# Delta stage attention: forget sums and causal mask added by TensorE in the score banks, and dummy products ahead of idle waits

## The chip, the cores and the metric

The kernel runs on one core of one Trainium2 chip. The metric is the device time of one execution in microseconds. TensorE (PE) multiplies, VectorE (DVE) and ScalarE (ACT) do the elementwise work, SyncE (SP) issues the DMAs. TensorE's clock is granted at one of two levels, 1.2 or 2.4 GHz; the profile gives it as a share of full speed.

## What is computed

Two transformers of two layers each, one behind the other, on 256 tokens of width 1024, all in float32. A layer of the first one has a mixer of three parts: a gated delta rule, a convolution and a "forgetting" attention of 6 heads. Layer 0 is followed by a dense feed-forward, layer 1 by eight experts of which each token takes two (the MoE stage). The second transformer has an attention with grouped heads (GQA) in its first layer and one with low rank projections (MLA) in its second. The part that the change rewrites is this attention:

```python
def forgetting_attention(q, k, v, log_f):
    c = jnp.cumsum(log_f.astype(f32), axis=1)
    ...
        s = jnp.einsum('bhqd,bhkd->bhqk', q_blk, kt) + cq_blk[..., None] - ck[:, :, None, :]
        s = jnp.where(key_pos[None, :] <= q_pos[:, None], s, -jnp.inf)
        p = jax.nn.softmax(s, axis=-1)
        return jnp.einsum('bhqk,bhkd->bqhd', p, vt)
```

To each score it adds the sum of the log forget gates from key to query, and it masks keys that lie behind the query.

## The kernel before

Each engine has one program, written out in order by hand; semaphores join them (`take` waits, `link` signals and waits for its own instruction). There is no scheduler: the order of the source is the order of the queue. Weights stream through a ring of six slots of 1 MB, which SP refills as the tiles that used a slot are done. PSUM is two tensors of four banks, `P0` (projections and attention outputs) and `P1` (everything else). A layer of the first transformer (`for l in range(2)`) runs on PE: 25 projection tiles `in`, mixed with transposes and Gram products of the delta rule; the inversion in five levels; the state loop of four chunks (from L799); `intra`; the turn of the delta rule's output (L831), which waits for DVE's `delta_out` (L1748) and is read by DVE at L1752 (`delta_read`); then `attention(FOX_PAIRS, ...)`, and the projection `out` (L497, called by `linear_normed`).

`attention` works on pairs of heads: six pairs, of which those with t = 0 have scores of width 128 (queries 0 to 127) and those with t = 1 of width 256. For pair p PE issues `scores(p)` (L608, two matmuls, one in rows 0 to 63 of the array and one in rows 64 to 127), `values(p-3)` (L618) and the transposes `flip(p-2)` (L627). DVE takes the row maximum of each of the two units (L1544), then moves an output (`put`, L1764), then divides the probabilities of pair p-1 (L1554, L1555). ACT takes the exponentials (L1113) and copies the turned probabilities out of PSUM (L1121). In the delta stage DVE's `prep` first adds the forget sums from `cc` and `CR` (L1759) and the mask `neg` (L1760) and writes the scores to SBUF (`SC`), from where the maximum and the exponential read them. In GQA and MLA the same `attention` has no `prep`: both read the bank.

`cc` (sums by query, a column for each head) and `CR` (sums by key, the same in all partitions) come from PE at L707 to L711 between the projection tiles, and DVE copies them at L1648 and L1649.

Elsewhere PE waits for a norm: for the standard deviation and the scaled rows (`rms_std`, then `both_ready` or `one_ready`) ahead of `gin`, `fup0`, `min` and `fup1`; for the last layer norm ahead of the squares that open the second transformer (`square_of`, L576); and for the routing table (`x_rows`, `row_map`) ahead of the gathers of the MoE stage (L877). The MoE stage streams its weights in 84 chunks of 4 MB into two buffers; chunk c+2 is issued when chunk c has been used.

In the profile a float32 matmul has two PE records, and a transpose one.

## Time and profile before

| | us |
|---|---|
| median of 3 runs | 3163.26 (3161.17 to 3167.71) |
| the profiled execution's own time | 3154.97 |
| its span | 3153.2 |
| mean granted TensorE clock | 0.962 of full speed |
| PE busy | 2884.5 (91%) |
| DVE busy | 1501.0 (48%) |
| ACT busy | 1137.2 (36%) |
| PE weight load busy | 1871.4 (59%) |

The span runs from the first to the last instruction. A busy PE is not a PE at its peak: its matmuls overlap, and at the lower clock the same work is busy for longer. The page gives the granted clock in 40 slices, which is too coarse for waits of some microseconds; the windows view gives it for any stretch.

### The profile page before, as it was taken

What the parts mean: (1) busy time and instruction counts of PE and PEld (TensorE: products, weight loads), DVE (VectorE), ACT (ScalarE), POOL (GpSimd) and SP (SyncE); (2) the same over time, 40 slices, a digit from 0 to 9 for tenths busy, and PEclk for the clock granted to TensorE, in tenths of its full rate; (3) what the DMA queues carried; (4) which work ended last, traced back from release to release, by engine and by line L of the source; (5) the groups of instructions that cost most, each with busy time, mean ns of one, the idle gap of its engine ahead of it and who ended that gap; (6) DMA issues with size and microseconds to landing.
All of it is one profiled execution on the core that took longest, in us unless ns stands there. A gap on an engine that the chain in (4) does not pass through costs nothing.

```text
span 3153.2 us, 67929 instructions
## 1 busy us (share of the span) xinstructions
PE 2884.5 (91%) x26308; PEld 1871.4 (59%) x26308; DVE 1501.0 (48%) x4806; ACT 1137.2 (36%) x3085; POOL 0.2 (0%) x4
## 2 busy tenths in 40 slices
PE   8979999978998989888988888989999999899998
PEld 7858887856555545555555554444444444557887
DVE  5641004564566666666666664783322200454321
ACT  3121002221566656565666652262211100243210
POOL 0000000000000000000000000000000000000000
PEclk9979999988999999999999998999999999999999
DMA  5444434364799999999999980101122211211441
GB/s 204 173 174 160 157 137 147 134 241 139 230 332 330 333 327 335 328 332 329 327 336 332 327 303 28 66 15 41 58 75 80 80 67 67 91 44 57 158 147 67
DMA packets 205858, 576.06 MB, mean 183 GB/s; under 512 B 6496, under 2 KB 6624, under 8 KB 179040
## 3 DMA queue, kind: packets, MB, share of 16 engines
q1 hardware_dynamic: 205536, 571.72, 52.5%
q8 instruction: 208, 3.41, 0.4%
q14 instruction: 114, 0.93, 0.1%
HBM read 570.65 MB, written 1.05 MB: 181 GB/s over the span
## 4 chain that ended last, share of the span: by engine, by line
PE 59%; DMA 21%; DVE 12%; issue 3%; ACT 3%; DVEq 1%; SPq 1%; ACTq 0%
PE P L497 44%; DMA ring<-ws_moe 20%; DVE arena L1894 4%; PE P L925 2%; DVE ring L1894 2%; PE P L686 1%; PE P L544 1%; PE P L608 1%; DVE small L1544 1%; PE P L618 1%; PE P L627 1%; DVEq L1891 1%; PE P L877 1%; PE P L576 1%; PE P L976 1%
## 5 line engine op out<-in xcount | busy, mean ns | idle before, releaser
L497 PE MATMUL P<-arena,ring 128*128 128x256 f32 (+1 forms) x2784 | 900.3, 484 | 24.7 <-ACT arena L1175 24.6
L497 PEld LDWEIGHTS P<-arena,ring 128*128 128x128 f32 x2784 | 531.9, 192 | 383.0 <-issue 335.4
L925 PE MATMUL P<-arena 128*32 128x256 f32 x6496 | 372.5, 381 | 6.0 <-DMA arena<-ws_moe 5.2
L925 PE MATMUL P<-ring,arena 128*32 128x256 f32 x4256 | 277.1, 409 | 75.6 <-DMA ring<-ws_moe 74.2
L497 PE MATMUL P<-X_sb,ring 128*128 128x256 f32 x1504 | 335.1, 384 | 2.2 <-ACT X_sb L1154 1.6
L497 PEld LDWEIGHTS P<-X_sb,ring 128*128 128x128 f32 x1504 | 287.5, 192 | 44.8 <-issue 3.1
L925 PEld LDWEIGHTS P<-arena 128*32 128x32 f32 x6496 | 215.0, 111 | 146.8 <-DMA arena<-ws_moe 9.7
L1894 DVE COPY arena<-ring 128x256 f32 x1008 | 211.6, 294 | 143.8 <-DMA ring<-ws_moe 138.8
L1377 ACT ACTIVATE arena<-ring 128x256 f32 x672 | 215.8, 406 | 170.0 <-DMA ring<-ws_moe 161.7
L925 PEld LDWEIGHTS P<-ring,arena 128*32 128x32 f32 x4256 | 148.7, 117 | 185.9 <-DMA ring<-ws_moe 86.7
L1894 DVE COPY arena<-arena 128x256 f32 x1008 | 211.8, 294 | 75.6 <-DMA arena<-ws_moe 58.4
L1377 ACT ACTIVATE arena<-arena 128x256 f32 x672 | 214.1, 403 | 72.9 <-DMA arena<-ws_moe 59.8
L925 PE MATMUL P<-arena,MIX 128*32 128x256 f32 x3360 | 192.0, 379 | 3.5 <-DMA arena<-ws_moe 2.9
L2038 DVE SCALAR_TENSOR_TENSOR arena<-P,pv,arena 128x510 f32<-128x510 f32 (+1 forms) x88 | 54.2, 616 | 290.1 <-ACT arena L1425 201.5
L1950 DVE SCALAR_TENSOR_TENSOR X_sb<-P,mod,X_sb 128x256 f32<-128x256 f32 x48 | 23.2, 484 | 296.7 <-PE P L497 296.1
L925 PE MATMUL P<-ring,MIX 128*32 128x256 f32 x2016 | 128.5, 402 | 37.5 <-DMA ring<-ws_moe 29.4
L925 PEld LDWEIGHTS P<-arena,MIX 128*32 128x32 f32 x3360 | 114.3, 110 | 73.3 <-issue 5.8
L497 PE MATMUL P<-MIX,ring 128*128 128x256 f32 (+1 forms) x512 | 147.1, 444 | 2.2 <-issue 2.2
L1894 DVE COPY ring<-ring 128x256 f32 x504 | 107.2, 294 | 68.0 <-DMA ring<-ws_moe 66.6
L1377 ACT ACTIVATE ring<-ring 128x256 f32 x336 | 108.8, 406 | 85.0 <-DMA ring<-ws_moe 80.2
L1165 ACT ACTIVATE arena<-X_sb 128x512 f32<-128x512 f32 (+1 forms) x40 | 21.0, 541 | 309.8 <-DVE X_sb L1950 309.8
L1894 DVE COPY ring<-arena 128x256 f32 x504 | 107.1, 294 | 47.1 <-DMA arena<-ws_moe 39.2
(360 smaller groups left out, 2652.6 us busy)
## 6 DMA issues: line engine op xcount, KB each, us to landing
ring<-ws_moe SPq DMA_DIRECT2D x84, 2048.0 KB, 14.2
arena<-ws_moe SPq DMA_DIRECT2D x84, 2048.0 KB, 15.2
ring<-ws_b SPq DMA_DIRECT2D x137, 1024.0 KB, 4.8
ring<-ws_a SPq DMA_DIRECT2D x67, 1024.0 KB, 4.9
cst_sb<-cst SPq DMA_DIRECT2D x1, 1664.0 KB, 8.5
X_sb<-xT SPq DMA_DIRECT2D x1, 1024.0 KB, 4.9
X_sb<-ctxT SPq DMA_DIRECT2D x1, 1024.0 KB, 4.7
out<-Y SPq DMA_DIRECT2D x2, 512.0 KB, 2.6
```

The lines of the kernel that those rows point to most:

```text
L497: ins = nc.tensor.matmul(bank(i, n), blockap(s, b % SLOT), rhs(kk), start=kk == 0, stop=kk == k - 1)
L544: ins = nc.tensor.matmul(P0[32 * j:32 * j + 32, b, 256 * half:256 * half + 256], csil[:, k, :], w, start=k == 0, stop=k == KD - 1)
L576: ins = nc.tensor.matmul(P1[:, 0, 0:n], c_("ones"), SQH[:, k, 0:n], start=k == 0, stop=k == KD - 1)
L608: nc.tensor.matmul(P1[:, (2 * p + i) % 4, 0:nk * P], q, kk, start=True, stop=True)\
L618: ins = nc.tensor.matmul(P0[i * HD:(i + 1) * HD, p % 2, 0:P], vfn(h + i, j), ptb[:, (2 * p + i) % 4, j * P:(j + 1) * P], start=j == 0, sto ...
L627: ins = nc.tensor.transpose(P0[:, 2 + i, j * P:(j + 1) * P], pb[:, (2 * p + i) % 6, j * P:(j + 1) * P], c_("ident"))
L686: ins = nc.tensor.matmul(P1[c:c + HD, 2 * i + h, r * HD:(r + 1) * HD], lhs[c:c + HD, g], cident[c:c + HD] if rhs is None else rhs[c:c + HD ...
L877: ins = nc.tensor.matmul(gathered(n)[:, 0:w], XTM[:, t, k * P:(k + 1) * P], SEL[:, t, at:at + w], start=t == 0, stop=t == TT - 1)
L925: ins = nc.tensor.matmul(acc(g // 2)[BR * j:BR * (j + 1), g % 2], x[:, b * BR:(b + 1) * BR], weights_of(b), start=k == 0, stop=last and kk ...
L1377: ins = a.activation(CB[u % 3][:, NDVE + j].rearrange("p (h c) -> p h c", h=2), src, ACT.Copy)
L1894: ins = v.tensor_copy(CB[u % 3][:, j].rearrange("p (h c) -> p h c", h=2), src)
L2038: L(v.scalar_tensor_tensor(f3[:, :, 1:], b3[:, :, 0:T - 1], pv[:, w0 + 3 * m:w0 + 3 * m + 1], f3[:, :, 1:], ALU.mult, ALU.add))
```

## The change

Four edits.

1. The forget sums and the mask go into the score banks on PE. Behind each score matmul, which no longer closes its accumulation, come a product of `ident` with `neg` on the last 128 columns and a product of two rows, `past_l` with `past_r`. The two rows are (-1, c of the query) and (c of the key, 1), so their product is c of the query less c of the key. DVE's `prep`, `SC`, `cc` and `CR` are gone, and maximum and exponential read the bank, as in GQA. The three small products for `cc` go, DVE copies 2 partitions in place of 128 for the key sums, and ACT makes the two operands from them with two activations of 2 x 1536 elements in the state loop.
2. The banks of this attention are rotated by two (`fox_bank`), so the first pair uses banks 2 and 3 of `P1`, and the scores of pair 0 are issued ahead of the turn of the delta rule's output, which moves into `attention` as `between`.
3. Unread products `busy(to, n)`: n matmuls of `ones` with `cos64`, 256 columns, into a part of a bank that nobody reads. They stand ahead of the waits for `delta_out` (6, in both layers), for the routing table (12), for the squares that open the second transformer (14), and for `rms_std` ahead of `gin` (10), `fup0` (10), `min` (10) and `fup1` (7).
4. Buffers in `arena` move to make room (not shown).

```diff
+        def fox_bank(u):
+            return P1[:, (u + 2) % 4]
...
+            def busy(to, n):
+
+                for _ in range(n):
+                    nc.tensor.matmul(to, c_("ones"), c_("cos64", T), start=True, stop=True)
...
-            def attention(pairs, qk, vfn, pb, ptb):
+            def attention(pairs, qk, vfn, pb, ptb, bias=None, between=None):
...
-                        nc.tensor.matmul(P1[:, (2 * p + i) % 4, 0:nk * P], q, kk, start=True, stop=True)\
-                            .then_inc(sem("scores"), 1)
+                        to = fox_bank(2 * p + i) if bias else P1[:, (2 * p + i) % 4]
+                        ins = nc.tensor.matmul(to[:, 0:nk * P], q, kk, start=True, stop=bias is None)
+                        if bias:
+                            ins = bias(to, h + i, t, nk)
+                        ins.then_inc(sem("scores"), 1)
...
                 for p in range(n + 3):
                     if p < n:
                         scores(p)
+                    if p == 0 and between:
+                        between()
...
-                nc.tensor.matmul(P1[:, 3, 0:6], c_("tri"), lft[:, 0], start=True, stop=True)
-                nc.tensor.matmul(P1[:, 3, 6:12], c_("tri"), lft[:, 1], start=True, stop=False)
-                nc.tensor.matmul(P1[:, 3, 6:12], c_("ones"), lft[:, 0], start=False, stop=True)
...
-                C.take("delta_out")
-                for r in range(6):
-                    ins = nc.tensor.transpose(P1[:, r // 3, r % 3 * P:(r % 3 + 1) * P],
-                                              O1[:, 2 * r:2 * r + 2, :].rearrange("p g d -> p (g d)"), c_("ident"))
-                ins.then_inc(sem("delta_flipped"), 1)
-                C.take("delta_read")
-                C.take("mod_ready", 6)
+
+                def forget(to, h, t, nk):
+
+                    nc.tensor.matmul(to[:, (nk - 1) * P:nk * P], c_("ident"), c_("neg"), start=False, stop=False)
+                    return nc.tensor.matmul(to[:, 0:nk * P], past_l[:, h, t * P:(t + 1) * P], past_r[:, h, 0:nk * P],
+                                            start=False, stop=True)
+
+                def delta_flip():
+
+                    for m in range(25 - NBANK, 25):
+                        if (TILE[f"in{l}"] + m) % NBANK == 3:
+                            wait_out(pe, TILE[f"in{l}"] + m)
+                    busy(P0[:, 3, 0:T], 6)
+                    C.take("delta_out")
+                    for r in range(6):
+                        ins = nc.tensor.transpose(P1[:, r // 3, r % 3 * P:(r % 3 + 1) * P],
+                                                  O1[:, 2 * r:2 * r + 2, :].rearrange("p g d -> p (g d)"), c_("ident"))
+                    ins.then_inc(sem("delta_flipped"), 1)
+                    C.take("delta_read")
+                    C.take("mod_ready", 6)
...
-                          lambda h, j: foxV[:, j, h * HD:(h + 1) * HD], foxP, foxPT)
+                          lambda h, j: foxV[:, j, h * HD:(h + 1) * HD], foxP, foxPT, forget, delta_flip)
...
+                    busy(P1[:, 0, T:2 * T], 12)
                     C.take("x_rows", 2)
...
+            busy(P1[:, 3, 0:T], 14)
             for k in range(KD):
                 x_wait(k)
...
             for l in range(2):
+                busy(P1[:, 1, 0:T], 10)
                 C.take("rms_std")
...
                     linear_squared("gout", KD, both(MIX), n)
+                    busy(P1[:, 1, 0:T], 10)
                     C.take("rms_std")
...
                     linear_squared("mout", KD, lambda k: mix1[:, k, :], T)
+                    busy(P1[:, 1, 0:T], 7)
                     C.take("rms_std")
...
+                    if n == 1:
+                        A.link(a.activation(past_r, past_l, ACT.Identity, scale=c_("ident", 1)[0:2], bias=second))
                     if n == 2:
+                        A.link(a.activation(past_l, past_l, ACT.Identity, scale=second, bias=less_first))
...
-                attention(FOX_PAIRS, lambda u, w: SC[:, u % 4, 0:w], foxP, foxPT)
+                attention(FOX_PAIRS, lambda u, w: fox_bank(u)[:, 0:w], foxP, foxPT)
...
-                L(v.tensor_copy(cc.rearrange("p t c -> p (t c)"), P1[:, 3, 0:12]))
-                L(v.tensor_copy(CR.rearrange("p h t -> p (h t)"), P1f[:, 0:1536]), "forget_read")
+                L(v.tensor_copy(past_l.rearrange("p h t -> p (h t)"), P1f[0:2, 0:1536]), "forget_read")
...
-                def prep(u, h, t, w):
-
-                    dst = SC[:, u % 4, 0:w]
-                    L(v.scalar_tensor_tensor(dst, P1[:, u % 4, 0:w], cc[:, t, h:h + 1], CR[:, h, 0:w], ALU.add, ALU.subtract))
-                    L(v.tensor_tensor(SC[:, u % 4, w - P:w], SC[:, u % 4, w - P:w], c_("neg"), ALU.add))
-                    return dst
-
-                attention(FOX_PAIRS, prep, foxP,
+                attention(FOX_PAIRS, lambda u, h, t, w: fox_bank(u)[:, 0:w], foxP,
```

PE in layer 0 from `intra` to the third pair's scores, before (L686 `intra`, L553 turns modulation rows, L831 turns the delta output, L608 scores, L627 `flip`):

```order
L686 MATMUL P<-arena 64x64 x24
L553 MATMUL P<-cst_sb,arena 128x96 x4
L831 MATMUL P<-cst_sb,arena 128x128 x6
L608 MATMUL P<-MIX 128x128 x2
L608 MATMUL P<-MIX 128x256 x2
L608 MATMUL P<-MIX 128x128 x2
L627 MATMUL P<-cst_sb,arena 128x128 x2
```

The same place now, up to the first unit of the second pair (L617 scores, L842 mask, L843 forget sums, L491 dummies, L854 the turn of the delta output):

```order
L699 MATMUL P<-arena 64x64 x24
L561 MATMUL P<-cst_sb,arena 128x96 x4
L617 MATMUL P<-MIX 128x128
L842 MATMUL P<-cst_sb 128x128
L843 MATMUL P<-arena 128x128
L617 MATMUL P<-MIX 128x128
L842 MATMUL P<-cst_sb 128x128
L843 MATMUL P<-arena 128x128
L491 MATMUL P<-cst_sb 128x256 x6
L854 MATMUL P<-cst_sb,arena 128x128 x6
L617 MATMUL P<-MIX 128x256
L842 MATMUL P<-cst_sb 128x128
```

The first pair's scores and the dummies now stand ahead of the turn, and between the two score matmuls of a pair stand a mask and a forget product.

DVE in the same stretch, before (L1748 writes `delta_out`, L1522 modulation, L1752 reads the turned output):

```order
L1748 TENSOR_TENSOR arena<-arena,small 128x768
L1522 TENSOR_TENSOR mod<-P,pv 128x2x3x2 x2
L1752 SCALAR_TENSOR_TENSOR MIX<-P,pv,Y 128x384 x2
L1759 SCALAR_TENSOR_TENSOR arena<-P,small,arena 128x128
L1760 TENSOR_TENSOR arena<-arena,cst_sb 128x128
L1544 TENSOR_REDUCE small<-arena 128x1
L1759 SCALAR_TENSOR_TENSOR arena<-P,small,arena 128x128
L1760 TENSOR_TENSOR arena<-arena,cst_sb 128x128
L1544 TENSOR_REDUCE small<-arena 128x1
```

And now:

```order
L1780 TENSOR_TENSOR arena<-arena,small 128x768
L1554 TENSOR_TENSOR mod<-P,pv 128x2x3x2 x2
L1784 SCALAR_TENSOR_TENSOR MIX<-P,pv,Y 128x384 x2
L1576 TENSOR_REDUCE small<-P 128x1 x4
L1586 RECIPROCAL small<-small 128x1
L1587 TENSOR_SCALAR arena<-arena,small 128x128
```

Of three instructions for a unit one is left; the four maxima of the first two pairs stand in a row.

## Rows read from the trace of the kernel before

**Rows 1.** Windows: stretch, length, busy by engine (records), granted clock, DMA share, GB/s.

```profile
194.12:221.05 26.93, 16.21 (x79) 9.13 (x79) 20.66 (x66) 9.69 (x36) 0.00 (x0) 0.50 0.00 1
221.05:231.30 10.25, 10.25 (x34) 8.50 (x35) 0.44 (x2) 0.00 (x0) 0.00 (x0) 0.70 0.00 0
722.12:731.30 9.18, 9.18 (x35) 7.84 (x36) 0.72 (x2) 0.00 (x0) 0.00 (x0) 0.81 0.00 0
```

**Rows 2.** Timeline, layer 0: start, duration, engine, line, operation, records [idle before <-releaser].

```profile
191.15 1.54 PE L831 MATMUL P<-cst_sb,arena 128*128 128x128 f32 x6 [4.62 <-DVE arena L1748]
192.79 1.27 DVE L1752 SCALAR_TENSOR_TENSOR MIX<-P,pv,Y 128x384 f32<-128x384 f32 x2 [1.29 <-PE P L831]
194.12 1.65 PE L608 MATMUL P<-MIX 64*128 64x128 f32 x8 [1.43 <-DVE MIX L1752]
...
200.73 0.35 DVE L1759 SCALAR_TENSOR_TENSOR arena<-P,small,arena 128x128 f32<-128x128 f32 x1
...
207.61 0.35 DVE L1759 SCALAR_TENSOR_TENSOR arena<-P,small,arena 128x128 f32<-128x128 f32 x1
...
221.05 10.20 PE L497 MATMUL P<-MIX,ring 128*128 128x256 f32 x32 [0.57 <-issue]
```

**Rows 3.** The chain that ended last, a stretch of projection tiles: start, length, records.

```profile
97.38 24.39 PE P L497 x112
```

**Rows 4.** Timeline, first work behind each wait; 1945.62 ends the first tile of `gin`.

```profile
785.38 13.05 PE L877 MATMUL P<-Y 128*128 128x512 f32 x32 [7.28 <-DVE Y L1842]
...
1922.25 9.49 PE L576 MATMUL P<-arena,cst_sb 128*128 128x512 f32 x16 [7.98 <-ACT arena L1165]
...
1937.60 16.01 PE L497 MATMUL P<-arena,ring 128*128 128x512 f32 x32 [5.85 <-ACT arena L1175]
...
1945.62 0.30 PEld L497 LDWEIGHTS P<-arena,ring 128*128 128x128 f32 x2 [0.88 <-ACT arena L1175]
...
2225.84 16.45 PE L497 MATMUL P<-arena,ring 128*128 128x512 f32 x32 [6.13 <-ACT arena L1175]
...
2695.14 4.03 PE L497 MATMUL P<-arena,ring 128*128 128x256 f32 x8 [6.13 <-ACT arena L1175]
...
2904.77 11.50 PE L497 MATMUL P<-arena,ring 128*128 128x256 f32 x40 [4.63 <-ACT arena L1175]
```

**Rows 5.** Groups by line, 194 to 221.1 us: count, busy us, mean ns, idle before.

```profile
L1759 DVE SCALAR_TENSOR_TENSOR arena<-P,small,arena 128x128 f32<-128x128 f32 (+1 forms) x12 | 5.0, 418 | 1.3 <-PE P L608 1.0
...
L1760 DVE TENSOR_TENSOR arena<-arena,cst_sb 128x128 f32<-128x128 f32 x12 | 3.5, 292 | 0.4
...
L1764 DVE TENSOR_SCALAR MIX<-P,pv 128x128 f32<-128x128 f32 x6 | 2.1, 351 | 3.2 <-PE P L618 3.1
```

**Rows 6.** Row maxima by tile (ns min/median/max), and score starts of the GQA attention, timeline.

```profile
L1544 DVE TENSOR_REDUCE small<-P x96: 424/691/693, 2056.0 to 2858.3; 128x1 f32<-128x512 f32 x64, 128x1 f32<-128x256 f32 x32
...
2070.42 1.13 PE L608 MATMUL P<-arena 64*128 64x512 f32 x4
...
2082.37 1.13 PE L608 MATMUL P<-arena 64*128 64x512 f32 x4
```

**Rows 7.** Timeline, forget sums of layer 0 and ACT rows near the new activations.

```profile
39.84 0.28 PE L707 MATMUL P<-small,cst_sb 128*128 128x6 f32 x2
...
40.43 2.82 PE L711 MATMUL P<-arena,cst_sb 128*128 128x512 f32 x6
...
41.74 0.84 ACT L1203 ACTIVATE arena<-arena 128x768 f32<-128x768 f32 x1
...
176.54 0.48 ACT L1294 ACTIVATE arena<-P 64x384 f32<-64x384 f32 x1 [6.46 <-PE P L807]
```

**Rows 8.** Window ahead of the issue of the fourth weight chunk of the MoE stage.

```profile
824.00:828.00 4.00, 4.00 (x80) 2.91 (x76) 4.00 (x21) 4.00 (x14) 0.00 (x0) 1.00 0.02 4
```

**Rows 9.** Windows in the routing of the MoE stage, columns as in rows 1.

```profile
775.60:776.10 0.50, 0.50 (x4) 0.50 (x3) 0.41 (x3) 0.00 (x0) 0.00 (x0) 0.50 1.13 324
...
777.00:778.00 1.00, 1.00 (x11) 0.92 (x10) 0.28 (x2) 0.97 (x2) 0.00 (x0) 1.00 0.99 268
```

More of the change, by code:

```diff
@@ L229, in build @@
         MT = [YD, bd(8)]
-        CR = arena_at(19968, 1536).rearrange("p (h t) -> p h t", h=H1)
+        past_l = arena_at(19968, 1536)[0:2].rearrange("p (h t) -> p h t", h=H1)
+        past_r = arena_at(0, 1536)[0:2].rearrange("p (h t) -> p h t", h=H1)
         foxA = FM.rearrange("p k r t -> p (k r t)")[:, 0:1536]
@@ L267, in build @@
         lft = small[:, 324:336].rearrange("p (t c) -> p t c", t=TT)
-        cc = small[:, 336:348].rearrange("p (t c) -> p t c", t=TT)
         rt = small[:, 352:512]
@@ L1566, in _ @@
             L(v.memset(rms_eps, RMS_EPS))
+            L(v.tensor_scalar(less_first, c_("ident", 1)[0:2], -1.0, None, ALU.mult))
             for g, ng in neg_gain.items():
```

6 lines of the change are left out of this document (3 added, 3 removed).

## The prediction

> **What bounds the kernel now.** PE is busy for 91% of the span, so the places matter in which it waits or runs at the low clock. First the windows view over the attention of the delta stage. In layer 0 it lasts 26.93 us from the first scores to the first matmul of `out`; DVE is busy for 20.66 us of it and PE for 16.21, and the granted clock is 0.50 throughout, which is 1.2 GHz [rows 1]; layer 1 issues the same instructions and is taken to be alike. The timeline shows why: PE had stood for 4.62 us before the turn of the delta output, then 1.43 us more, and every later burst is short [rows 2]. The `out` projection that follows runs its first 32 records in 10.20 us [rows 2], at a mean clock of 0.70, and in layer 1 the clock over that stretch is 0.81 [rows 1]. At full clock a 256 column record takes 24.39 / 112 = 0.218 us [rows 3], so 32 records would be 7.0 us.
>
> Then the waits of PE that get dummies, each with the work behind it [rows 4]. A low clock behind a wait costs time only where PE has its operands and runs dense work; where it waits for rows of the norm anyway it costs none.
>
> **The change part by part.**
>
> *Steady part of the attention.* From the third pair to the fifth DVE takes 207.61 - 200.73 = 6.88 us for two pairs, four units [rows 2], with next to no idle time in front of its groups [rows 5]. `prep` is 0.418 + 0.292 us a unit [rows 5], and about 0.78 with the gaps between instructions. Without it two pairs take 6.88 - 4 x 0.78 = 3.8 us, and with two `put` of 0.35 [rows 5], which that stretch does not yet hold, 4.5. The maximum now reads PSUM: 0.424 us for 256 elements [rows 6], where it was 0.42 from SBUF, so nothing there.
>
> PE gets for two pairs four mask products of 128 columns and four forget products, two of 128 and two of 256 columns. At full clock a matmul of two records is 0.22 us for 128 columns and 0.43 for 256 [rows 3]. The two score matmuls of a pair, which ran side by side in two halves of the array, now have others between them. That makes 1.1 us for a narrow pair's scores and 1.7 for a wide one's; with values (0.7) and transposes (0.7) some 4.2 us for two pairs at 2.4 GHz and 8.3 at 1.2 GHz. A product of only two rows is not in the trace. I price it like a full one; were it free, 1.3 us would go for two pairs, and it can't add more than its columns unless PSUM accumulation costs extra, which the long accumulations of `out` don't show.
>
> With DVE at 4.5 and PE at 4.2 neither is saturated, and what is late next is the loop across the engines: scores, two maxima, two exponentials, two copies, values, transposes, scores of the pair after next. I laid out the six pairs with the durations of the rows, each engine in its order. Scores of the odd pairs start at 0, 3.7 and 8.4 us behind the reading of the turned output, the last output is moved at 15.8 and `out` starts near 16.6 at full clock. The same layout gives 25.8 at 1.2 GHz, because PE is then the bound. Laid out for the kernel before it gives 26.4 where the trace has 26.93 [rows 1], and for four pairs of the GQA attention, which has no `prep`, 11.9 where the trace has 2082.37 - 2070.42 = 11.95 [rows 6]. So the gain lies between 1.1 and 10.3 us a layer. I take 8.6: nearly the full clock, since PE is busy 85% of the loop, with one stretch of some 3 us at the low one, most likely in the thin last 6 us.
>
> *The start.* PE now does the first scores and six dummies (1.1 + 6 x 0.43 = 3.7 us) ahead of `delta_out`, so 0.9 us of the 4.62 remain idle [rows 2], and the turn should be at full clock: its six records of 128 columns at 0.11 us in place of 0.22, some 0.85 us for 1.54 [rows 2, 3]. Gain 0.7 a layer, 1.4 in all; between 0 and 1.5.
>
> *`out` behind it.* Its low clock costs 3.2 us in layer 0 and, from 0.81 over 9.18 us [rows 1], 1.9 in layer 1. If the attention ends at full clock all 5.1 come back. The last 6 us are thin, so I take half: 2.6, between 0 and 5.1.
>
> *Forget sums.* L707 to L709 take 40.43 - 39.84 = 0.59 us of a busy PE [rows 7]: 1.1 in both layers, between 0 and 1.2. DVE's copy of 1536 elements stays as long with 2 partitions as with 128; its copy to `cc` was beside PE's work. ACT gets two activations of 1536 elements in each state loop. 768 took 0.84 us [rows 7], so 1.6 each. Behind them in ACT's queue is the copy L1294, which PE waits for in turn, but that copy stood idle for 6.46 us before [rows 7], so they cost nothing; uncovered they would be 6.4 us.
>
> *Dummies outside.* A dummy is 0.43 us at full clock. Ahead of the gathers 12 take 5.2 of 7.28 us; ahead of the squares 14 take 6.0 of 7.98; ahead of `gin` 10 take 4.3 of 5.85; ahead of `fup0` and `min` 4.3 of 6.13; ahead of `fup1` 7 take 3.0 of 4.63 [rows 4]. All fit if the clock is at 2.4 GHz when they start, and leave 1.5 to 2.1 us. What a full clock behind them gives: the gathers are 16 matmuls, half of 512 and half of 256 columns, 10.3 us for 13.05, gain 2.7. The squares are 16 records of 512 columns, 7.1 us for 9.49, gain 2.3. The 40 records of `fup1` take 11.50 for 8.9 at full clock, but at that clock its first tile would wait for rows of the norm, so of these 2.6 I take 1.7. In the first tile of `gin` PE, though it began at the low clock, stood 0.88 us for its last rows [rows 4], so a full clock gives nothing there, nor in `min`, whose matmuls are half as wide behind the same rows; in `fup0` I take 0.2. Sum 6.9, between 0 and 7.8.
>
> *Does it pass through the MoE stage?* It is bound by DMA later, but at its start the DMA engines stand (share 0.02) until chunk 1 is used [rows 8], so a PE that comes there earlier starts the stream earlier by as much.
>
> *Sum.* 17.2 + 1.4 + 2.6 + 1.1 + 6.9 = 29.2 us. Against the profiled execution's own 3154.97 that is 3125.8; the median of the runs shown lies 8.3 higher, so 3163.26 - 29.2 = 3134.
>
> **A rule weighed.** In the routing of the MoE stage PE ends a row of 16 transposes (L861) at a clock of 0.50, and a microsecond behind them, with only 8 column matmuls and four more transposes in between, the clock is 1.00 [rows 9]. So here transposes went ahead of a rise. The Trainium skill, "TensorE: Matmul & The Clock Gate", section "Part 4: PE-mode transpose", says that full speed does not engage for transposes and that they do not count as busy work in the same way. By that rule the turn and the `flip` records would not help to hold the clock in the attention, which makes rival A likelier; by the row they do. The trace disagrees with the rule, if one rise can; I leave a part of A's chance to it.
>
> **Rivals.**
>
> A. *PE takes DVE's place as the bound of the attention at 1.2 GHz.* The mask and forget products double PE's load, and the clock was 0.50 for the whole stretch. Against it: PE would then be busy nearly all the time, and in the trace dense work brings the clock up: the squares lose 9.49 - 7.1 = 2.4 us, five or six of their 16 records, and then run at full speed [rows 4]. Gain 2 x 1.1 + 1.1 + 1.4 + 6.9 = 11.6, so 3152.
>
> B. *The dummies don't hold the clock over the 1.5 to 2.1 us that remain,* or the products are not counted as they seem. Then the 6.9 are gone: gain 22.3, so 3141.
>
> C. *The MoE stage swallows what is saved ahead of it,* because its DMA would set its end from an earlier point. Only squares, `fup0` and `fup1` are left: 4.2, so 3159. Against it stands the idle DMA [rows 8].
>
> D. *Slower: dummies that run at 1.2 GHz outlast the waits they fill.* At 0.86 us each they take 12.0 us of 7.98 ahead of the squares, 10.3 of 7.28, 8.6 of 5.85, of 6.13 and of 6.13, 6.0 of 4.63: 4.1 + 3.0 + 2.7 + 2.5 + 2.5 + 1.4 = 16 us, and 2.5 in each attention, 21 in all. With the gains of A inside, 3.3, the kernel takes 3181. It decides from the point where a wait is shorter than its dummies, 9 low clock dummies for the squares. Against it: all these waits follow dense work, and at the one before the gathers the clock reads 1.00 a microsecond ahead [rows 9].
>
> **How the numbers follow.** Forecast 0.66 (with 0.04 for more than 35 us), A 0.10, B 0.17, C 0.04, D 0.03. A difference of 0.2%, 6.3 us, is about what a measurement of this kernel can tell from no change. Faster: forecast, A and B, 0.93; same: C, 0.04; slower: D, 0.03. The range: at best 2 x 10.3 + 1.5 + 5.1 + 1.2 + 7.8 = 36.2, so 3127, and 3 us for the scatter of the runs, 3124. Above it reaches over B and B with a weaker attention (gain 15), 3148; A, C and D, 0.17, are left out.
>
> **What would show it.** In the profile after: the first PE record of `out` 16.5 to 18.5 us behind the reading of the turned output; clock near 1.00 over most of it and DVE no longer continuous; the turn at 0.8 us; gathers near 10.3, squares near 7.1, the first 16 records of `fup1` with small gaps in them; 32 records of `out` between 7 and 10.2. A clock of 0.50 in the attention with PE busy without gaps speaks for A; 13.05 and 9.49 unchanged for B; the end of the MoE stage unmoved for C; first real matmuls later than `x_rows` or `rms_std` for D. The weakest step is how long the clock holds through the thin end of the attention.

## The result, and the profile after

The changed kernel is slower: 3177.97 us (median of 7 runs, 3168.98 to 3183.18) against 3165.18 for the kernel before in the same group of runs, a ratio of 1.0034 with an interval of [1.0023, 1.0046]. Forecast was 3134. Its profiled execution took 3183.01 us with a span of 3180.9; that is a long draw of after beside a short one of before (3154.97), so the two traces differ by 27.7 us where the medians differ by 12.8.

The page of the changed kernel: engines with busy time, share and instructions, and the granted clock in 40 slices.

```profile
PE 2961.9 (93%) x26542; PEld 1919.5 (60%) x26542; DVE 1483.4 (47%) x4757; ACT 1143.3 (36%) x3089; POOL 0.2 (0%) x4
...
PEclk9979999997999999999999999999999999999999
```

DVE lost 18 us of work, as meant, and PE gained 77 us. Where they went shows in the windows over the attention of layer 0, from the first scores behind the turn to `out`, over the first records of `out`, over the attention of layer 1, and over the "dummies" (the unread products of the change) and the gathers (columns as in [rows 1]).

```profile
197.03:235.17 38.14, 36.25 (x114) 20.61 (x115) 12.19 (x42) 9.64 (x36) 0.00 (x0) 0.51 0.00 0
...
235.17:245.00 9.83, 9.83 (x37) 8.31 (x38) 0.84 (x2) 0.00 (x0) 0.00 (x0) 0.80 0.01 2
705.00:743.60 38.60, 35.29 (x121) 20.23 (x119) 13.44 (x44) 9.69 (x36) 0.00 (x0) 0.57 0.00 1
...
800.70:808.45 7.75, 7.75 (x26) 6.36 (x25) 6.51 (x22) 0.00 (x0) 0.00 (x0) 0.68 1.02 336
808.45:818.80 10.35, 10.31 (x32) 5.73 (x31) 1.27 (x3) 2.45 (x5) 0.00 (x0) 1.00 0.67 231
```

The stretch that took 26.93 us [rows 1] takes 38.14. DVE's share fell from 20.66 to 12.19 us; PE is busy for 36.25, and the clock is 0.51 (0.50 before). The timeline of PE says what one unit costs (columns as in [rows 2]).

```profile
194.78 0.82 PE L854 MATMUL P<-cst_sb,arena 128*128 128x128 f32 x6
197.03 0.70 PE L617 MATMUL P<-MIX 64*128 64x256 f32 x2 [1.43 <-DVE MIX L1784]
197.66 0.49 PE L842 MATMUL P<-cst_sb 128*128 128x128 f32 x2
198.08 1.20 PE L843 MATMUL P<-arena 2*128 2x256 f32 x2
199.21 1.22 PE L617 MATMUL P<-MIX 64*128 64x256 f32 x2
200.36 0.79 PE L842 MATMUL P<-cst_sb 128*128 128x128 f32 x2
201.08 1.22 PE L843 MATMUL P<-arena 2*128 2x256 f32 x2
202.23 0.79 PE L617 MATMUL P<-MIX 64*128 64x128 f32 x2
202.95 0.79 PE L842 MATMUL P<-cst_sb 128*128 128x128 f32 x2
203.68 0.79 PE L843 MATMUL P<-arena 2*128 2x128 f32 x2
204.40 0.79 PE L617 MATMUL P<-MIX 64*128 64x128 f32 x2
```

The turn ran at full clock (0.82 us for 1.54 [rows 2]) and so did the first two products behind it. From 198.1 the starts are 1.15 us apart behind 256 columns and 0.72 behind 128, without an idle record. A wide unit, score, mask and forget product, costs 202.23 - 199.21 = 3.02 us, a narrow one 204.40 - 202.23 = 2.17. Its columns alone would be 2.1 us for a wide unit at this clock (products of 256, 128 and 256 columns, by the 0.436 us that 256 columns take at full clock, 24.39 / 56 [rows 3]); the other 0.9 us are three times 0.29, and a weight load (LDWEIGHTS) takes 0.30 us there. The stretch holds three wide and two narrow pairs, 3 x 6.04 + 2 x 4.34 = 26.8 us. With the values (L629, 5.5 us) and transposes (L638, 5.4 us), here from the groups by line of that stretch, this count gives 37.7 us, a little more than the 36.25 busy, since the first unit began at full clock. So PE's queue alone fills the attention.

```profile
L842 PEld LDWEIGHTS P<-cst_sb 128*128 128x128 f32 x20 | 4.8, 297 | 4.5 <-issue 4.5
L629 PE MATMUL P<-arena 128*64 128x128 f32 x36 | 5.5, 439 | 1.3 <-ACT arena L1150 1.3
L638 PE MATMUL P<-cst_sb,arena 128*128 128x128 f32 x18 | 5.4, 439 | 0.0
```

DVE now waits for it (its timeline).

```profile
202.41 0.42 DVE L1576 TENSOR_REDUCE small<-P 128x1 f32<-128x256 f32 x1 [2.60 <-PE P L843]
```

In the table "attention" runs from DVE's reading of the turned output to `out`; for the kernel before that is 221.05 - 192.79 = 28.3 [rows 2]. It follows the two traces by their landmarks.

| stretch | before, us | after, us | difference |
|---|---|---|---|
| start to the reading of the turned output, layer 0 | 192.8 | 195.7 | +2.9 |
| attention, layer 0 | 28.3 | 39.5 | +11.2 |
| `out` to the reading, layer 1 | 472.7 | 470.6 | -2.1 |
| attention, layer 1 | 28.3 | 37.8 | +9.5 |
| `out` to the gathers | 63.3 | 64.7 | +1.4 |
| gathers and the MoE stage | 1123.0 | 1129.2 | +6.2 |
| norm, squares, to `gin` | 29.3 | 28.6 | -0.7 |
| `gin` to `fup0` | 288.2 | 288.1 | -0.1 |
| `fup0` to `fup1` | 678.9 | 680.0 | +1.1 |
| `fup1` to the end | 248.4 | 246.7 | -1.7 |
| sum | | | +27.7 |

The attention is 20.7 of it. The MoE stage, whose code the change leaves as it is, took between 1119.5 and 1133.1 us in the fourteen traces of this study. Most of that lies between groups of runs: 1128.1 to 1133.1 us in the four traces of the first group of experiments, 1127.1 to 1130.5 in the four of the next, 1119.5 to 1123.6 in the three after that. The reading in layer 0 came at 192.8 to 196.1 us in the four traces whose kernels don't differ up to there. So the 6.2 and the first 2.9 are within what traces differ by anyway. That leaves 18.6 us, 4 more than the upper end of the interval (1.0046, 14.6 us); these 4 are not placed. One way would be that other executions of the changed kernel had the low clock for a shorter part of the attention, as one kernel below has in one layer and not in the other; there are no traces of them.

### The profile page after: what moved, and what is told of

The parts are those of the page before. It is cut to its first block, busy times and chain, and to the rows that moved or that the text cites. A ratio compares the mean times of both kernels' runs of the same rounds, so it can differ in the third digit from the quotient of the medians.

```text
span 3180.9 us, 68352 instructions
## 1 busy us (share of the span) xinstructions
PE 2961.9 (93%) x26542; PEld 1919.5 (60%) x26542; DVE 1483.4 (47%) x4757; ACT 1143.3 (36%) x3089; POOL 0.2 (0%) x4
## 4 chain that ended last, share of the span: by engine, by line
PE 60%; DMA 21%; DVE 11%; issue 3%; ACT 3%; DVEq 1%; SPq 1%; ACTq 0%
PE P L505 44%; DMA ring<-ws_moe 21%; DVE arena L1919 4%; PE P L950 2%; DVE ring L1919 2%; PE P L617 2%; PE P L699 2%; PE P L552 1%; PE P L629 1%; PE P L638 1%; DVEq L1916 1%; DVE small L1576 1%; PE P L584 1%; PE P L901 1%; PE P L1001 1%
## 5 line engine op out<-in xcount | busy, mean ns | idle before, releaser
L950 PE MATMUL P<-ring,MIX 128*32 128x256 f32 x2016 | 130.8, 407 | 35.9 <-DMA ring<-ws_moe 29.3
```

The costliest lines, as they stand in the source:

```text
L950: ins = nc.tensor.matmul(acc(g // 2)[BR * j:BR * (j + 1), g % 2], x[:, b * BR:(b + 1) * BR], weights_of(b), start=k == 0, stop=last and kk ...
```

## The experiments

The theory behind them: the loss is the price of the products in PE's queue, at a clock that they themselves keep low; the dummies outside are worth little. The rival: the dummies are a part of the loss.

**The dummies outside alone.** The kernel before with them (`busy` as in the change):

```diff
+                    busy(P1[:, 0, T:2 * T], 12)
                     C.take("x_rows", 2)
...
+            busy(P1[:, 3, 0:T], 14)
             for k in range(KD):
                 x_wait(k)
```

> The kernel before with only the dummies outside the delta stage's attention (12, 14, 10, 10, 10, 7), the attention untouched. Theory 1, the loss sits in the attention and the dummies outside bring a little: in the trace of the changed kernel the gathers bring 2.7 - 1.6 = 1.1 us (their dummies end 1.6 later than the wait did), the squares 0.7, fup1 1.8, the others 0, min and mout cost up to 1.5: 2.5 to 3.6 us faster than before, so about 3162 on the median 3165, and the MoE stage takes the 1085.0 us of before. Theory 2, the dummies are part of the loss, because the MoE stage behind the gathers took 1093.8 us in place of 1085.0: 5 us slower than before, with the same 1094 in its trace.

Measured: 3161.27 us, ratio 0.9977 [0.9965, 0.9988]. The rival, slower, is out. In the trace squares, `fup1` and `min` are as in the changed kernel. The gathers are not; here they are beside those of two later kernels (grouped order, and 128 rows in the order of the change):

```profile
779.57 5.37 PE L488 MATMUL P<-cst_sb 128*128 128x256 f32 x24
787.01 12.25 PE L882 MATMUL P<-Y 128*128 128x512 f32 x32 [2.07 <-issue]
...
785.43 10.56 PE L904 MATMUL P<-Y 128*128 128x512 f32 x32 [0.54 <-issue]
...
782.00 10.56 PE L902 MATMUL P<-Y 128*128 128x512 f32 x32 [2.06 <-issue]
```

With the dummies outside alone they ended 2.07 us ahead of the gathers and these took 12.25 us, little less than the 13.05 of [rows 4]. In the changed kernel the dummies ran at 0.68, took 7.75 us and ended as the gathers began, which then took 10.48. There the gathers started 1.4 us later behind the transposes of the routing than in the kernel before; the dummies make some 0.65 of it (the gathers began 0.75 us behind DVE's last write to `Y`, 0.10 before), the rest came with the small products of the routing, which ran slower (0.57 us for 0.37). These two traces alone would say that a set is worth 0.8 to 1.2 us, not 2.7. The later ones say more: where the dummies began at the low clock and ended 0.53 to 0.56 us ahead (four kernels) the gathers took 10.56 us with no delay behind DVE, and in one kernel they took 10.56 with the same 2 us of idle PE that cost the clock here. So the full gain did come in most kernels, and a gap of 2 us can go either way. The MoE stage took 1133.1 us here, so beside that stage the trace gives 2.3 us for all the dummies (gathers 0.8, squares 0.7, `fup1` 1.8, `gin` 0.1, less 1.1 between `fup0` and `fup1`, where those ahead of `min` stand), and the ratio 3.8 to 11; what is above 2.3 is not placed.

**The attention alone.** The changed kernel without any `busy`.

> The changed kernel without any of its dummies, inside and outside the attention. Theory 1: the attention is bound by PE at 1.2 GHz, 38 us in place of 27, so two layers cost 2 x 11 us, less 1.1 for the forget sums and about 1 for the earlier scores: 18 to 21 us slower than before, 3185; the turn is back at 1.5 us and the attention as long as with the six dummies, since with them the clock fell 1.4 us behind the first score anyway. Theory 2 (the dummies are part of the loss): under 12 us slower, 3174 or less.

Measured: 3189.88 us, ratio 1.0074 [1.006, 1.0087]: 23 us slower than before, where the first theory had 18 to 21 and the second under 12. The first is the nearer one, and misses by 2 us. Attention 40.3 us in both layers, the turn 1.51 us.

**The mask alone on PE.** The kernel before, with

```diff
+                            ins = nc.tensor.matmul(to[:, (nk - 1) * P:nk * P], c_("ident"), c_("neg"), start=False, stop=True)
...
-                    L(v.tensor_tensor(SC[:, u % 4, w - P:w], SC[:, u % 4, w - P:w], c_("neg"), ALU.add))
```

> The kernel before with the mask alone added by PE (ident times neg, 128 columns, behind each of the 12 score matmuls of a layer); DVE still adds the forget sums, and loses the 12 instructions of 0.29 us (0.33 with the gap). Theory 1, each product costs PE 0.72 us at 1.2 GHz in sequence (0.43 of columns and 0.29 that nothing hides): PE goes from 16.2 to 24.9 us busy in a layer, DVE from 20.7 to 17.2, and the attention stays between 26 and 29 us, the kernel within 4 us of before. Rival, only the product of two rows is dear: the attention follows DVE down to 23 to 24 us, the kernel 6 to 8 us faster.

Measured: 3178.4 us, ratio 1.004 [1.0024, 1.0055]. Attention 33.4 and 33.7 us, 5.2 more than before on average, though DVE was busy for 3.5 us less (17.16 for 20.66). Both missed: the rival by its sign, mine because it left out what the mask does to its neighbours. The two score matmuls of a pair, in the upper and the lower 64 rows, no longer follow each other and no longer run side by side: a narrow pair's two, 0.80 us in the trace of before, become 4 x 0.72 = 2.9 with their masks, a wide pair's 1.23 become 2 x (1.15 + 0.72) = 3.7. Three of each are 13.8 us more, and PE's busy time went from 16.21 to 30.04 us:

```profile
195.50:227.50 32.00, 30.04 (x102) 18.08 (x102) 17.16 (x54) 9.85 (x36) 0.00 (x0) 0.50 0.00 1
```

**A probe.** Unread products behind the last work of the kernel before, each row behind an idle PE; one execution.

```diff
+            at(2)
+            for i in range(24):
+                ins = mm(q[i % 4][:, 0:T], two_l, two_r, start=True, stop=True)
+            end(ins)
...
+            at(4)
+            for i in range(20):
+                mm(q[i % 4][:, 0:T], on_, mv, start=True, stop=True)
+            for i in range(10):
+                half_score(i, T)
+                mm(q[i % 4][:, P:T], id_, c_("neg"), start=False, stop=False)
+                ins = mm(q[i % 4][:, 0:T], two_l, two_r, start=False, stop=True)
```

> The kernel before with ten rows of unread products behind its last work, each behind an idle time of more than 4 us of PE (ACT copies 1536 elements four times), so only prices and clock are read: 24 full ones of 256 columns; 32 of 128 columns; 24 of two rows and 256 columns; ten times a unit of the changed attention (64 rows x 256, 128 x 128, 2 rows x 256); the same behind 20 full ones without a gap; the unit with its last product of 128 rows; 24 of 64 rows in alternate halves; 64 transposes; the units of two heads with the products of a kind next to each other; 20 full ones and then 24 of two rows. Theory a, the unhidden 0.29 us comes where the number of rows or the half of the array changes from one matmul to the next: full ones 0.43 us at full clock, two-row ones alone 0.43, 128 columns 0.22 to 0.25, the unit 1.15 + 0.72 + 1.15 = 3.0 at 1.2 GHz and 1.8 at 2.4; with 128 rows in the last product it loses one such piece, 2.7. Theory b, it belongs to every short product: 128 columns alone cost 0.42. For the clock, theory c: it doesn't rise through the unit nor through two rows alone, and falls to 0.50 in the unit that stands behind 20 full ones without a gap; rival d: it falls only behind an idle time, so behind the 20 full ones the unit runs at 1.00 throughout, and from a cold start it rises as with full ones.

Timeline: full products of 256 columns, of 128, two rows, 64 rows in alternate halves, transposes, and two-row ones behind 20 full ones.

```profile
3166.20 13.48 PE L1112 MATMUL P<-cst_sb 128*128 128x256 f32 x48 [7.23 <-ACT arena L1560]
3185.85 8.94 PE L1116 MATMUL P<-cst_sb 128*128 128x128 f32 x64 [6.17 <-ACT arena L1560]
3200.96 20.84 PE L1120 MATMUL P<-cst_sb 2*128 2x256 f32 x48 [6.17 <-ACT arena L1560]
...
3342.31 7.30 PE L1145 MATMUL P<-cst_sb 64*128 64x256 f32 x48 [6.17 <-ACT arena L1560]
3355.79 9.11 PE L1150 MATMUL P<-cst_sb 128*128 128x128 f32 x64 [6.19 <-ACT arena L1560]
...
3410.27 16.89 PE L1165 MATMUL P<-cst_sb 2*128 2x256 f32 x48
```

Windows of PE (length, busy, clock): two rows alone; ten units of the changed attention; the same behind full ones, in four stretches; units with 128 rows in the last product; halves at their end; transposes at their start and at their end; two-row ones behind full ones.

```profile
3200.96:3221.80 20.84, 20.84 (x48) 0.50 0.00 1
3227.98:3258.00 30.02, 30.02 (x60) 0.50 0.00 0
...
3274.80:3276.30 1.50, 1.50 (x7) 1.00 0.00 0
3276.30:3277.80 1.50, 1.50 (x7) 1.00 0.05 11
3277.80:3279.40 1.60, 1.60 (x4) 0.51 0.00 0
3279.40:3302.50 23.10, 23.10 (x47) 0.50 0.00 0
3308.80:3336.00 27.20, 27.20 (x60) 0.50 0.00 0
...
3347.00:3349.60 2.60, 2.60 (x26) 1.00 0.00 0
...
3355.80:3359.00 3.20, 3.20 (x15) 0.50 0.00 0
...
3362.00:3364.90 2.90, 2.90 (x27) 1.00 0.00 0
...
3414.00:3427.00 13.00, 13.00 (x32) 0.51 0.00 0
```

On the clock, theory c holds and d falls. Two-row products never brought it up in 20.84 us of unbroken work, and behind full ones, with no gap, it was lost. The unit of the changed attention does the same. Full products, 64-row ones in alternate halves and transposes bring it up. On the price, theory a holds and b falls: 128 columns on the full array cost 8.94 / 32 = 0.28 us with their cold start, while the unit cost 3.02. But one part was not expected: the unit with 128 rows in its last product (2.72 us) stays at 0.50 too. With the products of a kind next to each other a wide pair costs 4.31 us, where the order of the change costs 6.04.

**Grouped order.** The changed kernel, with scores, masks and forget products of a pair each next to each other:

```diff
+                    for i in range(2):
+                        nc.tensor.matmul(to[i][:, (nk - 1) * P:nk * P], c_("ident"), c_("neg"), start=False, stop=False)
+                    for i in range(2):
+                        nc.tensor.matmul(to[i][:, 0:nk * P], past_l[:, h + i, t * P:(t + 1) * P], past_r[:, h + i, 0:nk * P],
+                                         start=False, stop=True).then_inc(sem("scores"), 1)
```

> The changed kernel with its products in another order: for a pair the two scores, then the two masks, then the two forget products, in place of score, mask, forget for the one head and then for the other. In the probe that order took 4.31 us for a pair of 256 columns where the changed order takes 2 x 3.02 = 6.04, both at 1.2 GHz. Theory, the loss comes from products that no longer run beside each other or hide their weight loads: 3 wide pairs save 1.73 each and 3 narrow ones about 1.2, 8.8 us a layer, so from the reading of the turned output to out 30 to 31 us in place of 39.5, the clock still 0.50 (the two rows are still there), and the kernel 17 us faster than the changed one, near 3161. Rival, the time is set by the clock alone and other engines take over as the limit: less than 4 us a layer.

Measured: 3155.94 us, ratio 0.9966 [0.9951, 0.9981]. Attention 26.8 us in layer 0, where the clock was 1.00 up to 200 us, and 31.7 in layer 1, where it was 0.63 from 691 to 695 us and 0.50 behind; the text expected 30 to 31 in both. The order of PE's products alone turns the change from 0.34% slower into 0.34% faster.

**DVE's share.** The kernel before with the mask put into the key sums beforehand, so `prep` is one instruction:

```diff
-                    L(v.scalar_tensor_tensor(dst, P1[:, u % 4, 0:w], cc[:, t, h:h + 1], CR[:, h, 0:w], ALU.add, ALU.subtract))
-                    L(v.tensor_tensor(SC[:, u % 4, w - P:w], SC[:, u % 4, w - P:w], c_("neg"), ALU.add))
+                    L(v.scalar_tensor_tensor(dst, P1[:, u % 4, 0:w], cc[:, t, h:h + 1], CR[:, h] if t else CRM[:, h],
+                                             ALU.add, ALU.subtract))
```

> The kernel before with the mask already in the sums that DVE subtracts: one DVE instruction for a unit in place of two, 12 of 0.33 us fewer in a layer; two DVE instructions of 768 elements in the state loop, in waits of 1.8 and 2.8 us. PE does what it did before. Theory, DVE bounds the attention of before: 28.3 us from the reading to out become 24.4 to 25, the kernel 7 us faster than before, 3159. Rival, the loop across the engines sets it at the low clock and DVE's share only fills it: 27 us or more, under 3 us faster.

Measured: 3152.68 us, ratio 0.9949 [0.9932, 0.9965]; attention 24.5 in both layers, 3.8 less each. So DVE did bound the attention of the kernel before, as the prediction read it, and the forecast of the attention failed on PE's side. The ratio says 11 us or more where the attention gives 7.6 (the text expected 7 in all); another 1.5 lie between `out` of layer 0 and the reading in layer 1, the rest is not placed.

**One product of 128 rows, and more dummies.** Grouped, with mask and forget sums in one product; `CR` and `CRM` hold the mask less the key sums:

```diff
+                    for i in range(2):
+                        nc.tensor.matmul(to[i][:, 0:nk * P], c_("ident"), CR[:, h + i] if t else CRM[:, h + i],
+                                         start=False, stop=True).then_inc(sem("scores"), 1)
```

> The changed kernel with all its dummies, but one product of 128 rows for mask and forget sums together (ident times a matrix that holds the mask less the key sums; the query's own sum is the same for a whole row and leaves the softmax as it is), the two scores of a pair next to each other and then the two products. DVE makes the matrices with three instructions of 768 elements in the state loop. Theory c, the clock follows how many rows of the array work: with no two-row product and the 64-row ones side by side it rises in the attention as it did in the probe for 64 rows in alternate halves and for transposes; reading to out 18 to 21 us, the last part of it near 1.00, out 7 to 9 us, the kernel 15 to 20 us faster than before, 3148. Rival, PE's waits decide and the clock stays 0.50: PE then needs 16.2 + 3 x (1.15 + 2.0) = 25.7 us a layer, reading to out 27 to 29, the kernel within 4 us of before.

Measured: 3132.6 us, ratio 0.9886 [0.9869, 0.9902]. Attention 19.8 us in both layers, the clock back at 1.00 from 205.6 us, `out` 7.14 us for its 32 records, which is full speed. The attention is as the text had it; the kernel gained 36 us, twice the 15 to 20 expected, of which the attention has 17.0 and `out` 4.8. The windows are a stretch at the low clock, the rest of the attention from where the clock is back, and `out`:

```profile
198.50:200.40 1.90, 1.90 (x5) 1.11 (x4) 0.42 (x1) 0.62 (x5) 0.00 (x0) 0.50 0.00 0
...
205.60:216.30 10.70, 8.37 (x70) 5.29 (x69) 7.90 (x28) 5.43 (x22) 0.00 (x0) 1.00 0.00 0
216.30:223.50 7.20, 7.20 (x34) 6.35 (x35) 0.45 (x2) 0.00 (x0) 0.00 (x0) 1.00 0.01 2
```

> As the kernel with one product of 128 rows for mask and forget sums, and with more dummies: 3 in the wait for the reading of the turned output and 13 in the attention, ahead of waits for exponentials and turned probabilities. Theory c: where the clock falls in the waits of the kernel without them, these hold it at 1.00 to the end, reading to out 17 to 19 us and out at 7.0, some 3 us a layer better than without. If the clock isn't held, they cost 16 x 0.86 = 14 us a layer at 1.2 GHz less the idle time they fill: reading to out over 30 us, slower than before.

Measured: 3139.64 us, ratio 0.991 [0.9893, 0.9927]. The clock is 1.00 from the reading to the end of `out`, and the attention is 20.7 us, 0.8 longer than with 0.50 in most of its first half, where the text had 17 to 19. The dummies did hold the clock, and they stood ahead of real work. The two effects part in the trace of the kernel without the dummies ahead of `gin`, `fup0` and `min` (below), whose attention is the same code as that with one product. In its layer 0 the clock stayed at 1.00, in its layer 1 it fell:

```profile
193.08:210.52 17.44, 13.52 (x95) 8.40 (x95) 13.45 (x44) 8.37 (x36) 0.00 (x0) 1.00 0.01 4
679.34:699.19 19.85, 16.20 (x95) 10.11 (x95) 13.44 (x44) 8.51 (x36) 0.00 (x0) 0.83 0.01 2
```

So a held clock was worth 2.4 us in a layer, and the 16 further dummies, with the waits moved for them, cost 3.2.

**Rows alone, in both orders.** The forget product over 128 rows, 126 of them zeros, all else as it was: first with the grouped order, then with the order of the change.

```diff
-                        nc.tensor.matmul(to[i][:, 0:nk * P], past_l[:, h + i, t * P:(t + 1) * P], past_r[:, h + i, 0:nk * P],
+                        nc.tensor.matmul(to[i][:, 0:nk * P], past_l_all[:, h + i, t * P:(t + 1) * P], past_r_all[:, h + i, 0:nk * P],
```

> The kernel with scores, masks and forget products grouped by kind, and the forget product over 128 rows in place of two: the same two rows and zeros in the other 126, in both operands (cleared by two memsets of DVE). The columns, the number and the order of PE's products are the same. Theory c, the clock follows the rows in use: it rises in the attention, which had 0.50 from 203 us on, and reading to out comes from 31.7 us (layer 1) to 22 to 25, out from 9.5 towards 7.1; the kernel 12 to 18 us faster than with two rows. Rival, it is the number and size of the products and the idle time between them: 0.50 as before, 30 to 32 us less the 0.29 a pair that an equal tile shape saves between mask and forget product, at most 1.8 us a layer.

Measured: 3124.43 us, ratio 0.9884 [0.9869, 0.9899], so 0.8% or 26 us from two rows to 128, beyond the 12 to 18 expected. Attention 19.2 and 20.8 us for 26.8 and 31.7, `out` 7.14 in both layers for 9.79 and 9.49: 23.5 us together. Layer 0 in windows:

```profile
196.00:199.00 3.00, 2.97 (x21) 2.23 (x21) 2.49 (x10) 1.68 (x9) 0.00 (x0) 1.00 0.01 3
199.00:202.00 3.00, 3.00 (x25) 2.09 (x25) 1.90 (x7) 1.57 (x6) 0.00 (x0) 1.00 0.00 0
202.00:205.00 3.00, 3.00 (x24) 1.95 (x24) 2.08 (x8) 1.14 (x6) 0.00 (x0) 1.00 0.00 0
```

The same products with two rows had 0.58 from 200 to 203 us and 0.50 behind. In PE's queue columns, number, order and waits are the same, and only the rows differ; DVE has two memsets more, ahead of the attention. So the clock follows the rows in use here. Equal rows of mask and forget product also save one unhidden 0.29 us a pair, which this pair of kernels doesn't part from the rows. The probe does: its two-row products by themselves take their columns and no more (20.84 / 24 = 0.87 us), and the clock stays down.

> The changed kernel with the forget product over 128 rows (126 of them zeros) and nothing else changed: the products of a pair stay in its order, score, mask, forget for the one head and then for the other. With the changed kernel, the grouped one and the grouped one with 128 rows this makes four cases, order by rows. By the probe the unit in this order costs 2.72 us at 1.2 GHz with 128 rows in its last product, and the clock did not rise in ten of them: so 0.50 stays, and a unit saves 0.30: reading to out 34 to 36 us, the kernel 6 us faster than the changed one, slower than or as fast as before, 3168. Rival, rows alone are enough in the kernel, since transposes and values stand between the units and the clock is at 1.00 when the first unit starts: 1.00 in most of the attention, reading to out 22 to 25 us, 30 us faster than the changed one, 3145.

Measured: 3149.48 us, ratio 0.9955 [0.9929, 0.9981]. Each text has one layer: layer 0 took 22.6 us, as the rival said, and layer 1 took 36.6, as the theory did (34 to 36) to within 1 us, both with six dummies ahead and the same instructions:

```profile
198.00:201.00 3.00, 3.00 (x15) 1.83 (x15) 1.75 (x6) 1.77 (x8) 0.00 (x0) 1.00 0.01 3
...
684.00:700.00 16.00, 16.00 (x47) 9.46 (x45) 5.41 (x19) 4.75 (x20) 0.00 (x0) 0.51 0.00 0
```

Its ten runs fall into clusters: three from 3128 to 3131 us, one at 3141, five from 3149 to 3152, one at 3159. In layer 1 the clock, once lost, didn't come back before `out`, which cost 14.0 us; that two, one or no such layer in a run explains the clusters is what one trace suggests, not what is shown.

**Fewer dummies.** The kernel with one product, without those ahead of `gin`, `fup0` and `min`, and without any.

> The kernel with one product of 128 rows for mask and forget sums, without the dummies ahead of gin, fup0 and min. By the trace of the kernel before with only the outside dummies these three bring nothing and the ones ahead of min cost 1.1 us: 1 us faster than with them, which the median can't show, 3131.6. Rival, they hold a clock that the work behind needs: 2 us slower or more.

> The same kernel without any dummies. Theory: the attention brings its own clock up, because after three pairs it is dense enough; only the turn (0.7 us a layer) and the outside dummies (2.7 us) are lost and some 1 us a layer in the first pairs: 6 us slower than with all dummies, 3139. Rival, the start at full clock is what lets the clock come back early: 0.50 to the end of the attention, 27 us from reading to out and out at 9.5 us, 20 us slower, 3153.

Measured: 3130.4 us, ratio 0.9909 [0.9896, 0.9923], and 3132.6 us, ratio 0.9912 [0.9898, 0.9925], beside the 3124.43 of the 128-row kernel in the same group of runs. Without the three sets it is as expected (3131.6), a difference that the runs can't show; without any, 3139 were expected. Without any dummies the attention is 18.9 us in both layers and its clock comes up by itself, in layer 0 as follows; `out` has 7.14 and 8.82 us, the gathers 13.04.

```profile
194.00:197.20 3.20, 3.17 (x10) 1.69 (x10) 1.01 (x3) 1.04 (x5) 0.00 (x0) 0.50 0.00 0
197.20:198.80 1.60, 1.60 (x9) 1.38 (x9) 1.30 (x5) 0.90 (x4) 0.00 (x0) 0.55 0.00 0
198.80:211.50 12.70, 10.45 (x80) 6.46 (x78) 9.91 (x35) 6.52 (x28) 0.00 (x0) 1.00 0.00 1
```

The kernel with the four sets left and the one with none lie 2.2 us apart in one group of runs, which can't be told from nothing. The one with all of them stands at 0.9886 [0.9869, 0.9902] in another group, 0.0026 or 8 us lower, with an interval that just touches. By the same comparison the three sets ahead of `gin`, `fup0` and `min` would be worth 7 us, where the trace of the outside dummies has them as a loss of 1 us, so two groups of runs may differ by as much. What all the dummies are worth is not shown, beyond that from end to end of the intervals it is at most 18 us.

| kernel | attention, layers 0 and 1, us | ratio to before |
|---|---|---|
| before | 28.3, 28.3 | 1 |
| changed: its order, 2 rows | 39.5, 37.8 | 1.0034 |
| its order, 128 rows | 22.6, 36.6 | 0.9955 |
| grouped, 2 rows | 26.8, 31.7 | 0.9966 |
| grouped, 128 rows | 19.2, 20.8 | 0.9884 |
| grouped, one product of 128 rows | 19.8, 19.8 | 0.9886 |
| the same without three sets of dummies | 17.4, 19.9 | 0.9909 |
| the same without any | 18.9, 18.9 | 0.9912 |

The grouped kernels with 128 rows beat the kernel before by 0.9 to 1.2%, and keep what the change wanted of DVE in the attention.

## Why the prediction was wrong

**The steady part of the attention** carried 17.2 of the 29.2 us, and its sign was wrong: +20.7. Two steps of it failed.

The price of a product. The text took 0.22 and 0.43 us, the columns alone, and for a wide pair 1.7 us at 2.4 GHz, so 3.4 at 1.2; the trace has 6.04. It had seen that the two score matmuls of a pair "now have others between them", but its sums don't hold it: 0.43 + 0.44 + 0.86 = 1.7, and 0.22 + 0.44 + 0.44 = 1.1 for a narrow pair, count the two scores once, as if still side by side. One after the other they make 2.2 and 1.3, or 4.3 for a wide pair at 1.2 GHz. And it had no term for the loading of weights. Between these products of unlike rows it shows: 0.29 us a product at 1.2 GHz, six of them in a pair, 1.7 us. So "it can't add more than its columns" was false, and for the 25.8 us of the layout at 1.2 GHz the trace has 38.14. A hint was within reach: the first two pairs' scores took 1.65 us [rows 2], where their columns, side by side at 1.2 GHz, make 0.43 + 0.85 = 1.28.

The clock. The text saw 0.50 throughout [rows 1] and argued that a PE busy for 85% of the loop would bring it up, from the squares, which use the full array. Busy time alone isn't the measure: with 36.25 us busy of 38.14 it stayed at 0.51. How many rows PE computes with in that time matters, and the two-row product that the text would "price like a full one" isn't one for the clock. Of the two steps this one turned the sign. In the order of the change, with 128 rows, the layer that kept 1.00 took 22.6 us, so the price by itself left 5.7 us of gain where 8.6 were forecast; the rest, to 39.5, is the clock, with the little that 128 rows save in price. And where both were mended, one grouped product and the clock at 1.00, the attention took 17.4 us, within the 16.5 to 18.5 that the prediction named: the layout across the engines was sound.

**The start**: the turn took 0.82 us as forecast, but the first pair's scores with their masks and forget products took 2.5 us ahead of it, not 1.1. So the dummies ended 0.5 us behind `delta_out`, and the reading starts 0.2 us earlier, not 0.7. **`out`**: 9.1 and 9.2 us for 32 records for 10.2 and 8.8, gain 0.8 in place of 2.6. **Forget sums**: right, 0.6 us a layer (L721 starts 8.9 us behind the end of the first 48 records, where L711 started 9.5 behind them). **Dummies outside**: 6.9 forecast, 2.7 in the trace of the change and 2.3 in that of the dummies alone. `fup1` was right (1.8). The squares gained 0.7 of 2.3 (8.80 us for 16 records), with 1.93 us between the last dummy and them. The gathers are told above. Between `fup0` and `fup1`, where those ahead of `min` stand, 1.1 were lost, where the text had a gain of 0.2.

**The MoE stage** did pass on what came later or earlier at its start, as far as its scatter of 14 us lets one see. That scatter is larger than most terms of the sum, and the text took the profiled run of before, its shortest, as if the 8.3 us between it and the median were a constant.

**The rivals.** A named the right thing, PE as the bound at 1.2 GHz, and gave it 0.10 and a gain, since its price came from the same wrong layout. B was right in the main for the squares, in all traces, and for the gathers in the trace of the outside dummies alone. D, dummies that outlast the wait, came true ahead of the gathers in the changed kernel, for some 0.65 us in place of 3.0, and ahead of `delta_out`, for 0.5 in place of 2.5. No rival had PE's products themselves as a loss; the slower side was built from the dummies only.

**The rule weighed.** The trace goes against it more clearly now: 64 transposes behind an idle PE start at 0.50 and end at 1.00 in the probe. That full speed does not engage for them (the Trainium skill, "TensorE: Matmul & The Clock Gate", "Part 4: PE-mode transpose") doesn't hold here. Its result, rival A's clock, did come, but from the products of few rows. The two-row ones do it alone. The unit with 128 rows in its last product stayed at 0.50 too; whether its lone 64-row products do that or the unhidden weight loads between unlike products, no run parts.

## What to carry to other kernels

Price a small product by what stands next to it: here products that use other rows of the array than their neighbour took 0.29 us more at 1.2 GHz, and a product put between two half-array ones undid their overlap; so group by kind. Ask of work moved to PE how much of the array it fills, and fill it with zeros if need be: two rows cost the time of 128 and here also half the clock. And dummies that hold the clock stand in the same queue: here a held clock was worth 2.4 us a layer and the dummies that held it cost 3.2.

## What the runs showed of the hardware

- Two-row products of 256 columns ran 20.84 us at 0.50 without a gap, and brought 1.00 down behind full ones. In the grouped attention, whose clock fell with them, the same ones with zeros in 126 more rows kept it at 1.00 in layer 0: rows of zeros count.
- A matmul of 256 columns behind one of the same rows takes 0.44 us at full clock (24.39 / 56 [rows 3]), and 0.87 at 1.2 GHz with two rows (20.84 / 24). In a row score (64 rows), mask (128), forget (2) each takes 0.29 us more than its columns at 1.2 GHz, and with 128 rows in the last 0.10 less on average (2.72 for 3.02).
- Transposes and 64-row matmuls in alternate halves bring the clock from 0.50 to 1.00 behind 6.2 us of idle PE, in rows of 9.11 and 7.30 us.
- The same instructions can run at either clock in two layers of one execution, 22.6 us and 36.6, or 17.4 and 19.9 for the grouped ones.
